# Two experts per engine loop turn on TensorE, buffers fixed by the expert's parity, extra passes behind expert 1

## The chip, the cores and the metric

One core of one Trainium2 chip runs the whole kernel. The metric is the device time of that core in microseconds (us), from one execution of the program. A run of this kernel repeats within 0.1%, so a median of a few runs tells changes of about 0.2% apart.

## What is computed

A decoder layer for 256 tokens of width 2048: a gated mixer over the sequence (two large projections, `a_w_in` 2048 x 4096 and `a_w_out` 2048 x 2048), then a mixture of 32 experts in 4 groups, then a final RMSNorm. All of it is float32. The mixture is the part that matters here:

```python
def hier_moe(h, w_group, b_group, w_exp, b_exp, w_gate, w_up, w_down):
    ...
    e_w, e_idx = lax.top_k(jax.nn.softmax(e_logits, axis=-1), TOP_K)      # TOP_K = 2
    ...
    def run_block(args):
        rows, e = args
        xb = x_pad[rows]
        return (jax.nn.silu(xb @ w_gate[e]) * (xb @ w_up[e])) @ w_down[e]
```

Each token goes to two of the 32 experts. An expert has three weight matrices of 2048 x 512 or 512 x 2048 float32, 4 MB each, 12 MB in all; the 32 experts have 384 MB, and each byte is used once.

## The kernel before

The program is written engine by engine; each engine has its own list of instructions and waits on named semaphores.

**Phase 1**, up to about 300 us, computes the mixer, with its weights split into a high and a low part, and then the router. TensorE's part of it holds one engine loop (`pe.Fori`, L1080) of two turns with two column blocks each.

**Phase 2** goes through the experts 0 to 31 in order. Each expert takes up to `CAP` = 32 tokens. On TensorE, `gather(e)` picks the tokens of the expert with a one-hot matrix, `transpose_xe(e)` turns them round, `gate_up(e)` multiplies them with gate and up weights in two halves, `transpose_gu(e)` turns the result, `down(e)` multiplies it with the down weights in two halves, and `scatter(e, t)` spreads the result over the tokens, one call for each of the two tiles of tokens. The gather of expert e+1 and the scatter of expert e-1 stand between the parts of expert e. ScalarE copies results out of PSUM, VectorE scales them and adds them to `acc`.

**The weights** come in chunks of 2 MB, six per expert and 192 in all: chunks 0 to 3 of an expert are gate, up, gate, up (two halves of the rows), chunks 4 and 5 are down. They are issued in order on one queue, SP's (`load_chunk`, L277). There are ten buffers of 2 MB (`slot`), and chunk 9 is put in the not yet used `acc`. `chunk_at(i)` gives the buffer of chunk i, and how many chunks have been in it before: from chunk 11 on the ten buffers are used in turn. SP waits before a load until TensorE has used the chunk that lay in the buffer before; the semaphore is one of four, counted by expert:

```python
e, c = divmod(i - NSLOT - (1 if i < IN_ACC + 1 + NSLOT else 0), NCH)
sp.wait_ge((gu_half, gu_half, gu_ps, gu_ps, y_half, y_ps)[c], e + 1)
```

`gu_half` and `gu_ps` come from TensorE at the end of the first and the second half of `gate_up`, `y_half` and `y_ps` at the end of the halves of `down`.

**Extra passes.** An expert with more than 32 tokens gets the rest in extra passes, whose number is known only at run time. GpSimd counts them, VectorE lists them (`list_passes`, L944), then TensorE, ScalarE and VectorE read the number and branch round the loop of passes if it is zero, as it is with these inputs. This stands behind expert `BREAK` - 1 = 15. There the pipeline of experts is emptied: `expert_run(0, BREAK)` ends with both scatters of expert 15, and `expert_run(BREAK, NEXP)` starts with the gather of expert 16, where elsewhere the gather of the next expert comes before `down`.

Of the kernel before, what the change touches and what calls it, by code (L numbers as in the profile page):

```python
# [20 lines left out]
def hybrid_layer(nc, x, norm_mix, norm_ffn, norm_final, w_in, ln_g, ln_b, w_s, b_s, w_out,  # L21
# [22 lines left out]
    IN_ACC = 9  # L44
    NCHUNK = NCH * NEXP

    MAXX = 16
    BREAK = NEXP // 2
    XUSED = 2 * KD + FT * NB
    XIN = 16 * XUSED  # L50
    assert (NT, KD, NB, FT, NQ, GD, NGRP * EPG, FE) == (2, 16, 4, 4, 4, 256, NEXP, 512)
# [1 line left out]
    with ExitStack() as ctx:  # L53
# [166 lines left out]
                return w[0, e, a * D // 2:(a + 1) * D // 2, :].rearrange("(p k) n -> p k n", k=8)  # L220
            return e_down[0, e, (c - 4) * 256:(c - 3) * 256, :].rearrange("(p b) n -> p b n", b=2)

        def chunk_at(i):

            if i < IN_ACC:
                return i, 0
            if i == IN_ACC:
                return NSLOT, 0
            if i == IN_ACC + 1:
                return NSLOT - 1, 0  # L230
            n = i - (IN_ACC + 2)
            return n % NSLOT, n // NSLOT + 1

        def chunk_tile(i):
            where = (slot + [acc[:, :, :].rearrange("p t d -> p (t d)")])[chunk_at(i)[0]]
            return where[:, :].rearrange("p (k n) -> p k n", k=8 if i % NCH < 4 else 2)

        def wait_chunk(pe, i):
            s, before_it = chunk_at(i)
            pe.wait_ge(chunk_in[s], 16 * (before_it + 1))  # L240
            if i in (IN_ACC + 2, IN_ACC + 3):
                pe.wait_ge(first_part[i - IN_ACC - 2], 16)

        def extra_passes(eng, body):

# [22 lines left out]
        @block.sync  # L268
        def _(sp):
            def load_half(src, n, hc, fresh=False):  # L270

                if not fresh:
                    sp.wait_ge(lo_done, HC * n + hc - 3)
                sp.dma_start(w_raw[:, hc % 4, :, :], src).then_inc(raw_in[hc % 4], 16)

            def load_chunk(i):
                sp.dma_start(chunk_tile(i), expert_chunk(i)).then_inc(chunk_in[chunk_at(i)[0]], 16)  # L277

            for q in range(NB):
                cols = slice(q * NBLK, (q + 1) * NBLK)  # L280
                sp.dma_start(h[:, :, cols], x[0, :, cols].rearrange("(t p) d -> p t d", p=P)).then_inc(x_in[q], 16)
                load_half(w_in_half(D, q), 0, q, fresh=True)

            for n in range(2 * NB):
                col = D + n * NBLK if n < NB else (n - NB) * NBLK
                for hc in range(4 if n == 0 else 0, HC):
                    load_half(w_in_half(col, hc), n, hc)
                if 1 <= n <= 3:
                    load_chunk(n - 1)
                if n == NB + 2:  # L290
                    sp.wait_ge(ln_done, NT * NB)
                    load_chunk(3)
                if n == NB + 3:
                    load_chunk(4)
            for n in range(NB):
                for hc in range(HC):
                    load_half(w_out_half(n * NBLK, hc), 2 * NB + n, hc)
                if n == 0:
                    sp.wait_ge(yt_ps, KD // 2)
                    load_chunk(5)  # L300
                if n == 1:
                    load_chunk(6)
            sp.wait_ge(w_used, 3 * NB * HC - HC // 2)
            load_chunk(7)
            sp.wait_ge(lo_done, 3 * NB * HC)
            load_chunk(8)
            sp.wait_ge(w_used, 3 * NB * HC)
            load_chunk(9)
            load_chunk(10)

            sp.wait_ge(gu_quarter, 1)
            for i in (IN_ACC + 2, IN_ACC + 3):
                half = 1 if i % NCH >= 4 else 4
                sp.dma_start(chunk_tile(i)[:, 0:half, :], expert_chunk(i)[:, 0:half, :]
                             ).then_inc(first_part[i - IN_ACC - 2], 16)
            sp.wait_ge(gu_half, 1)
            for i in (IN_ACC + 2, IN_ACC + 3):
                half = 1 if i % NCH >= 4 else 4
                sp.dma_start(chunk_tile(i)[:, half:2 * half, :], expert_chunk(i)[:, half:2 * half, :]
                             ).then_inc(chunk_in[chunk_at(i)[0]], 16)  # L320
            for i in range(IN_ACC + 4, NCHUNK):

                e, c = divmod(i - NSLOT - (1 if i < IN_ACC + 1 + NSLOT else 0), NCH)
                sp.wait_ge((gu_half, gu_half, gu_ps, gu_ps, y_half, y_ps)[c], e + 1)
                if i < NCHUNK - 1:
                    load_chunk(i)
                else:
                    for b in range(2):
                        sp.dma_start(chunk_tile(i)[:, b, :], expert_chunk(i)[:, b, :]
                                     ).then_inc((chunk_in[chunk_at(i)[0]], last_in)[b], 16)  # L330
            sp.wait_ge(gu_ps, NEXP - 1)
            sp.dma_start(g_final, norm_final.rearrange("(a d) -> a d", a=1).partition_broadcast(P)).then_inc(final_in, 16)

            for t in range(NT):
                for j in range(2):
                    sp.wait_ge((out_ready, out_ready_act)[j], t + 1)
                    cols = slice(j * D // 2, (j + 1) * D // 2)
                    sp.dma_start(out[0, t * P:(t + 1) * P, cols], acc[:, t, cols]).then_inc(out_stored, 16)
            sp.wait_ge(out_stored, 16 * NT * 2)
# [674 lines left out]
        def _(pe):  # L1014
# [172 lines left out]
            pe.matmul(R[:, COUNTS], ones_bf[:, :], mask[:, 1, :], start=False, stop=True).then_inc(ranks_ps, 1)  # L1187
            keep_busy(3)

            def gather(e):  # L1190
                if e == 0:
                    pe.wait_ge(sel_first, 1)
                else:
                    pe.wait_ge(sel_ready, e + 1)
                    pe.wait_ge(scatT_ready, e)
                for t in range(NT):
                    if e == 0 and t == 1:
                        pe.wait_ge(sel_ready, 1)
# [2 lines left out]
                                        start=(t == 0), stop=(t == NT - 1))  # L1201
                ins.then_inc(xe_ps, 1)

            def transpose_xe(e):
                pe.wait_ge(xe_ready, e + 1)
                if e:
                    pe.wait_ge(xeT_ready, e)
                for b in range(KC):
                    ins = pe.transpose(TRX[:, b * P:(b + 1) * P], xe.rearrange("p (c k) -> p k c", k=KC)[:, b, :],  # L1209
                                       ident[:, :])  # L1210
                ins.then_inc(xeT_ps, 1)
                pe.wait_ge(scat_ready, e + 1)
                for t in range(NT):
                    ins = pe.transpose(XE[:, t * P:(t + 1) * P], scat[:, t, :, :].rearrange("p q c -> p (q c)"), ident[:, :])
                ins.then_inc(scat_ps, 1)

            def gate_up(e):
                pe.wait_ge(xeT_ready, e + 1)
                if e:
                    pe.wait_ge(hT_ready, e)  # L1220
                for a in range(2):
                    tiles = [chunk_tile(NCH * e + 2 * a), chunk_tile(NCH * e + 2 * a + 1)]
                    wait_chunk(pe, NCH * e + 2 * a)
                    wait_chunk(pe, NCH * e + 2 * a + 1)
                    for k in range(8):
                        for c in range(NQ):
                            ins = pe.matmul(GU[c * CAP:(c + 1) * CAP, 0:256], xeT[:, k % KC, 2 * a + k // KC, :],  # L1227
# [3 lines left out]
                            ins.then_inc(gu_quarter, 1)  # L1231
                    ins.then_inc((gu_half, gu_ps)[a], 1)

            def transpose_gu(e):
                pe.wait_ge(gu_ready, e + 1)
                for b in range(2):
                    ins = pe.transpose(TRG[:, b * P:(b + 1) * P], gu.rearrange("p (c b) -> p b c", b=2)[:, b, :],
                                       ident[:, :])
                ins.then_inc(tr_ps, 1)

            def down(e):
                pe.wait_ge(hT_ready, e + 1)
                if e:
                    pe.wait_ge(y_ready, e)
                for c in range(2):
                    i = NCH * e + 4 + c
                    wait_chunk(pe, i)
                    for b in range(2):
                        if i == NCHUNK - 1 and b == 1:
                            pe.wait_ge(last_in, 16)  # L1250
# [3 lines left out]
                                            start=(c == 0 and b == 0), stop=(c == 1 and b == 1))  # L1254
                    ins.then_inc((y_half, y_ps)[c], 1)

            def scatter(e, t):
                if t == 0:
                    pe.wait_ge(y_ready, e + 1)
                    pe.wait_ge(scatT_ready, e + 1)  # L1260
                if NT * e + t:
                    pe.wait_ge(acc_done, NT * e + t)
                for j in range(NB):
                    rows_j = slice(j * CAP, (j + 1) * CAP)
                    ins = pe.matmul(O[j], scatT[rows_j, e % 2, t, :], y_sb[rows_j, :], start=True, stop=True)  # L1265
# [9 lines left out]
                        pe.matmul((O, O_LAST)[t][j][:, :], scatT[rows_j, e % 2, t, :], y_sb[rows_j, :],  # L1275
                                  start=True, stop=True).then_inc(scattered, 1)

            def expert_run(lo, hi):
                gather(lo)
                transpose_xe(lo)  # L1280
                for e in range(lo, hi):
                    gate_up(e)
                    if e > lo:
                        scatter(e - 1, 0)
                    if e + 1 < hi:
                        gather(e + 1)
                    transpose_gu(e)
                    if e + 1 < hi:
                        transpose_xe(e + 1)
                    if e == NEXP - 1:  # L1290
                        scatter(e - 1, 1)
                    down(e)
                    if e > lo and e < NEXP - 1:
                        scatter(e - 1, 1)
                if hi < NEXP:
                    scatter(hi - 1, 0)
                    scatter(hi - 1, 1)
                else:
                    last_scatter(hi - 1)

            def extra_pass(i):
                pe.wait_ge(x_sel, i + 1)
# [40 lines left out]
                    ins.then_inc(x_scattered, 1)  # L1343

            pe.sem_inc(x_used, 1)
            expert_run(0, BREAK)
            pe.wait_ge(passes_ready, 1)
            extra_passes(pe, extra_pass)
            expert_run(BREAK, NEXP)


# [20 lines left out]
```

## Time and profile before

| | |
|---|---|
| median of 3 runs | 1239.74 us (1239.44 to 1240.37) |
| the profiled execution | 1239.77 us |
| its span, first to last instruction | 1238.0 us |
| TensorE matmuls busy | 930.7 us, 7775 matmuls and as many weight loads |
| VectorE, ScalarE, GpSimd busy | 378.5, 223.3, 28.4 us |
| mean granted TensorE clock | 0.868 of full speed |
| moved by DMA | 462.33 MB, mean 373 GB/s |

The profile lists instructions by engine with start and duration, DMA traffic by queue, and the chain of waits that ended last. Times within it count from the first instruction; 1.8 us of the execution lie outside the span. A stretch of the profile can be asked for with its own numbers, so that a queue or an engine can be read for some microseconds alone.

### The profile page before, as it was taken

The page shows a single profiled execution, that of the slowest core. Times are in us where ns is not written, and L with a number is a line of the kernel's source. Part 1 is how long each engine was busy: PE and PEld are TensorE (multiplying, and loading weights), DVE is VectorE, ACT ScalarE, POOL GpSimd, SP SyncE. Part 2 cuts the span into 40 slices and gives each one's busy share as a digit, 9 for nine tenths or more (in the row PEclk, how much of TensorE's full clock was granted, in tenths as well). Part 3 has the DMA queues.
Part 4 walks back from the last instruction along what each step waited for, and adds up shares of the span by engine and source line. Part 5 has one row for each costly group of instructions (what it writes and reads, how often), then busy time and mean ns, then how long its engine had stood idle before and what let it go on. Part 6 is the DMA issues. An engine that isn't in the chain of part 4 may idle for free.

```text
span 1238.0 us, 17396 instructions
## 1 busy us (share of the span) xinstructions
PE 930.7 (75%) x7775; PEld 526.7 (43%) x7775; DVE 378.5 (31%) x479; ACT 223.3 (18%) x380; POOL 28.4 (2%) x60
## 2 busy tenths in 40 slices
PE   7999999999976767767777763866676667666674
PEld 6788788887433333333333321322233323322331
DVE  4554746445222222222222214222222222222214
ACT  5644555434100000000000000100000000000003
POOL 1100000000200000000000000000000000000003
PEclk9999999999997887887787886978878878888877
DMA  8877567857999999999999999999999999999993
GB/s 261 320 251 264 186 212 256 297 171 276 373 426 427 427 427 426 427 428 427 426 427 427 426 428 425 425 429 427 426 428 427 427 428 424 428 427 427 427 418 128
DMA packets 56811, 462.33 MB, mean 373 GB/s; under 512 B 4984, under 2 KB 5088, under 8 KB 31392
## 3 DMA queue, kind: packets, MB, share of 16 engines
q1 hardware_dynamic: 56000, 458.25, 90.6%
q0 software_dynamic: 656, 2.94, 0.7%
q8 instruction: 62, 1.02, 0.3%
q14 instruction: 13, 0.11, 0.0%
q10 hardware_dynamic: 80, 0.02, 0.0%
HBM read 459.09 MB, written 2.10 MB: 373 GB/s over the span
## 4 chain that ended last, share of the span: by engine, by line
DMA 55%; PE 39%; ACT 2%; DVE 2%; POOL 1%; issue 1%; POOLq 0%; SPq 0%; ACTq 0%; DVEq 0%
DMA slot<-in_e_w_up 54%; PE scattered_out L1049 19%; PE bank L1227 8%; PE bank L1252 5%; PE bank L1200 2%; PE scattered_out L1265 1%; PE bank L1209 1%; DMA w_raw<-in_a_w_out 1%; ACT arena L581 1%; POOL h L416 1%; DVE w_lo L680 1%; ACT w_hi L430 1%; PE bank L1093 1%; DMA w_raw<-in_a_w_in 0%; PE bank L1139 0%
## 5 line engine op out<-in xcount | busy, mean ns | idle before, releaser
L1227 PE MATMUL bank<-slot,arena 128*32 128x256 f32 x4064 | 343.8, 511 | 248.3 <-DMA slot<-in_e_w_up 247.1
L1227 PEld LDWEIGHTS bank<-slot,arena 128*32 128x32 f32 x4064 | 186.5, 145 | 415.0 <-issue 382.5
L922 DVE TENSOR_TENSOR acc<-scattered_out,acc 128x2048 f32<-128x2048 f32 x60 | 137.5, 2292 | 638.1 <-PE scattered_out L1265 638.1
L680 DVE TENSOR_TENSOR w_lo<-w_raw,w_hi 128x1024 fp32r<-128x1024 f32 x96 | 118.8, 1238 | 129.9 <-ACT w_hi L430 129.7
L1049 PE MATMUL scattered_out<-w_hi,xT_first 128*128 128x512 f32 x384 | 126.7, 400 | 3.4 <-DVE xT_first L689 1.9
L430 ACT CAST w_hi<-w_raw 128x1024 fp32r<-128x1024 f32 x96 | 100.9, 1051 | 138.0 <-PE scattered_out L1049 130.6
L1049 PE MATMUL scattered_out<-w_hi,xT_second 128*128 128x512 f32 x376 | 122.0, 396 | 0.5 <-DVE w_lo L680 0.5
L1252 PE MATMUL bank<-slot,arena 128*32 128x512 f32 x1024 | 116.5, 595 | 2.2 <-DVE arena L916 2.2
L591 ACT COPY arena<-bank 128x256 f32<-128x256 f32 x32 | 11.9, 372 | 563.5 <-PE bank L1227 563.5
L1049 PEld LDWEIGHTS scattered_out<-w_hi,xT_first 128*128 128x128 f32 x384 | 72.8, 190 | 22.1 <-issue 2.8
L1049 PEld LDWEIGHTS scattered_out<-w_hi,xT_second 128*128 128x128 f32 x376 | 70.6, 188 | 17.1 <-DVE w_lo L680 0.9
L1265 PE MATMUL scattered_out<-arena 32*128 32x512 f32 x496 | 71.7, 648 | 6.9 <-DVE acc L922 6.9
L1049 PE MATMUL scattered_out<-w_lo,xT_first 128*128 128x512 f32 x192 | 75.6, 394 | 0.0
L1049 PE MATMUL scattered_out<-w_lo,xT_second 128*128 128x512 f32 x188 | 73.4, 390 | 0.0
L1200 PE MATMUL bank<-h,arena 128*32 128x512 f32 x512 | 62.9, 610 | 13.4 <-issue 13.4
L1252 PEld LDWEIGHTS bank<-slot,arena 128*32 128x32 f32 x1024 | 30.0, 109 | 65.6 <-issue 62.1
L602 ACT COPY arena<-bank 128x512 f32<-128x512 f32 x32 | 18.7, 585 | 177.5 <-PE scattered_out L1265 163.6
L1049 PEld LDWEIGHTS scattered_out<-w_lo,xT_first 128*128 128x128 f32 x192 | 36.5, 190 | 6.7
L1265 PEld LDWEIGHTS scattered_out<-arena 32*128 32x128 f32 x496 | 19.6, 185 | 45.4 <-issue 40.0
L1049 PEld LDWEIGHTS scattered_out<-w_lo,xT_second 128*128 128x128 f32 x188 | 35.4, 188 | 6.3
L1200 PEld LDWEIGHTS bank<-h,arena 128*32 128x32 f32 x512 | 13.8, 110 | 56.9 <-issue 55.7
L581 ACT COPY arena<-bank 128x512 f32<-128x512 f32 x32 | 18.7, 585 | 99.4 <-PE bank L1200 99.4
(176 smaller groups left out, 416.6 us busy)
## 6 DMA issues: line engine op xcount, KB each, us to landing
slot<-in_e_w_gate SPq DMA_DIRECT2D x63, 2048.0 KB, 39.9
slot<-in_e_w_up SPq DMA_DIRECT2D x63, 2048.0 KB, 44.3
slot<-in_e_w_down SPq DMA_DIRECT2D x62, 2048.0 KB, 39.1
w_raw<-in_a_w_in SPq DMA_DIRECT2D x64, 512.0 KB, 4.0
w_raw<-in_a_w_out SPq DMA_DIRECT2D x32, 512.0 KB, 4.2
slot<-in_e_w_down SPq DMA_DIRECT2D x4, 1024.0 KB, 25.0
h<-in_x SPq DMA_DIRECT2D x4, 512.0 KB, 7.2
acc<-in_e_w_up SPq DMA_DIRECT2D x1, 2048.0 KB, 10.3
```

Source lines behind the costliest of these rows:

```text
L416: pool.tensor_tensor(h[:, t, cols], acc[:, t, cols], g_final[:, cols], ALU.mult).then_inc(acc_g_done, 1)
L430: act.copy(w_hi[:, hc % 2, :, :], w_raw[:, hc % 4, :, :]).then_inc(hi_done, 1)
L581: act.copy(xe, XE[:, :]).then_inc(xe_ready, 1)
L602: act.copy(y_sb, Y[:, :]).then_inc(y_ready, 1)
L680: dve.tensor_tensor(w_lo[:, hc % 2, :, :], w_raw[:, hc % 4, :, :], w_hi[:, hc % 2, :, :].bitcast(F32), ALU.subtract).then_inc(lo_done, 1)
L922: dve.tensor_tensor(acc[:, t, :], OUT[:, :], (acc if e else h)[:, t, :], ALU.add).then_inc(acc_done, 1)
L1049: ins = pe.matmul(Z[parity][t][:, :], a(k)[:, toks], b[:, hc % 2, j, :], start=(k == 0 and part == 0), stop=(k == KD - 1 and part == 2))
L1093: ins = pe.matmul(X[i % 4][:, j * GD:(j + 1) * GD], ws_T[:, g + j, :], v[:, t, (g + j) * GD:(g + j + 1) * GD], start=True, stop=True)
L1200: ins = pe.matmul(XE[j * CAP:(j + 1) * CAP, :], sel[:, e % 2, t, :], gather_columns(t, j), start=(t == 0), stop=(t == NT - 1))
L1227: ins = pe.matmul(GU[c * CAP:(c + 1) * CAP, 0:256], xeT[:, k % KC, 2 * a + k // KC, :], tiles[c // 2][:, k, (c % 2) * 256:(c % 2 + 1) * 25 ...
L1252: ins = pe.matmul(Y[j * CAP:(j + 1) * CAP, :], hT[:, b, c * CAP:(c + 1) * CAP], chunk_tile(i)[:, b, j * NBLK:(j + 1) * NBLK], start=(c == ...
L1265: ins = pe.matmul(O[j], scatT[rows_j, e % 2, t, :], y_sb[rows_j, :], start=True, stop=True)
```

## The change

- TensorE's experts 4 to 29 become an engine loop (`pe.Fori`) of 13 turns with two experts each. The waits in it count from registers (`2 * m + ...`). Experts 0 to 3, 30 and 31 stay written out.
- For that every turn must name the same buffers: from chunk 12 on, the six chunks of an even expert lie in the buffers 1, 2, 3, 4, 5, 6 and those of an odd one in 7, 8, 9, 0, 5, 6. Both take their down chunks in 5 and 6. SP waits for the last chunk that lay in the same buffer.
- `BREAK` becomes 2: the extra passes, and the emptied pipeline round them, stand behind expert 1 on all three engines.

SP's list stays written out, and the order of the chunks stays. The core of the diff:

```diff
-    BREAK = NEXP // 2
+    LOOP, LAST_LOOP = 4, 30
+    EVEN_SLOTS, ODD_SLOTS = (1, 2, 3, 4, 5, 6), (7, 8, 9, 0, 5, 6)
+    BREAK = 2
...
+        def buffer_of(i):
+            if i < IN_ACC:
+                return i
+            if i == IN_ACC:
+                return NSLOT
+            if i == IN_ACC + 1:
+                return NSLOT - 1
+            if i == IN_ACC + 2:
+                return 0
+            return (EVEN_SLOTS, ODD_SLOTS)[i // NCH % 2][i % NCH]
+
+        earlier = [[j for j in range(i) if buffer_of(j) == buffer_of(i)] for i in range(NCHUNK)]
+
         def chunk_at(i):
-            if i < IN_ACC:
-                return i, 0
...
-            n = i - (IN_ACC + 2)
-            return n % NSLOT, n // NSLOT + 1
+            return buffer_of(i), len(earlier[i])
...
-                e, c = divmod(i - NSLOT - (1 if i < IN_ACC + 1 + NSLOT else 0), NCH)
+                e, c = divmod(earlier[i][-1], NCH)
                 sp.wait_ge((gu_half, gu_half, gu_ps, gu_ps, y_half, y_ps)[c], e + 1)
...
+            def wait_chunk(i, m=0):
+                s, before_it = chunk_at(i)
+                per_turn = 16 if i % NCH < 4 else 32
+                pe.wait_ge(chunk_in[s], per_turn * m + 16 * (before_it + 1))
...
-            def gate_up(e):
-                pe.wait_ge(xeT_ready, e + 1)
+            def gate_up(e, m=0):
+                pe.wait_ge(xeT_ready, 2 * m + (e + 1))
...
-            def expert_run(lo, hi):
...
+            def other_experts():
+                gather(BREAK)
+                transpose_xe(BREAK)
+                for e in range(BREAK, LOOP):
+                    expert(e, first=(e == BREAK))
+                with pe.Fori(0, (LAST_LOOP - LOOP) // 2) as m:
+                    expert(LOOP, m=m)
+                    expert(LOOP + 1, m=m)
+                for e in range(LAST_LOOP, NEXP):
+                    expert(e, last=(e == NEXP - 1))
+                last_scatter(NEXP - 1)
...
-            expert_run(0, BREAK)
+            first_experts()
             pe.wait_ge(passes_ready, 1)
             extra_passes(pe, extra_pass)
-            expert_run(BREAK, NEXP)
+            other_experts()
```

The order of instructions shows two places. The first is SP's queue at the down chunks of experts 3 and 4; each row is one load of 2 MB with the semaphore that it waits for. Before:

```order
40 L277 DMA slot0<-in_e_w_up 128x4096 [waits y_ps]
41 L277 DMA slot1<-in_e_w_down 128x4096 [waits gu_half]
42 L277 DMA slot2<-in_e_w_down 128x4096 [waits gu_half]
43 L277 DMA slot3<-in_e_w_gate 128x4096 [waits gu_ps]
44 L277 DMA slot4<-in_e_w_up 128x4096 [waits gu_ps]
45 L277 DMA slot5<-in_e_w_gate 128x4096 [waits y_half]
```

The same place after the change:

```order
40 L280 DMA slot0<-in_e_w_up 128x4096 [waits y_ps]
41 L280 DMA slot5<-in_e_w_down 128x4096 [waits y_half]
42 L280 DMA slot6<-in_e_w_down 128x4096 [waits y_ps]
43 L280 DMA slot1<-in_e_w_gate 128x4096 [waits gu_half]
44 L280 DMA slot2<-in_e_w_up 128x4096 [waits gu_half]
45 L280 DMA slot3<-in_e_w_gate 128x4096 [waits gu_ps]
```

Row 40 is chunk 21, the last of the gate and up chunks of expert 3, and is the same in both. Row 41 is chunk 22. It waited for the first half of `gate_up(2)`, and waits now for the first half of `down(2)`; all later loads stand behind it.

The second place is TensorE behind `down` of expert 1 (`chunk_in9` and `chunk_in0` are its two down chunks). Before:

```order
904 L1252 MATMUL bank<-slot,arena 32x512 [waits chunk_in9,y_ready,hT_ready]
905 L1252 MATMUL bank<-slot,arena 32x512 x7
906 L1252 MATMUL bank<-slot,arena 32x512 [waits first_part0,chunk_in0]
907 L1252 MATMUL bank<-slot,arena 32x512 x7
908 L1265 MATMUL scattered_out<-arena 128x512 [waits acc_done]
909 L1265 MATMUL scattered_out<-arena 128x512 x3
910 L1227 MATMUL bank<-slot,arena 32x256 [waits first_part1,chunk_in1,chunk_in2,hT_ready,xeT_ready]
```

The same place after the change:

```order
900 L1262 MATMUL bank<-slot,arena 32x512 [waits first_part0,chunk_in0]
901 L1262 MATMUL bank<-slot,arena 32x512 x7
902 L1275 MATMUL scattered_out<-arena 128x512 [waits acc_done]
903 L1275 MATMUL scattered_out<-arena 128x512 x3
904 L1275 MATMUL scattered_out<-arena 128x512 [waits acc_done,scatT_ready,y_ready]
905 L1275 MATMUL scattered_out<-arena 128x512 x3
906 L1275 MATMUL scattered_out<-arena 128x512 [waits acc_done]
907 L1275 MATMUL scattered_out<-arena 128x512 x3
908 L249 TENSOR_LOAD n_extra_i [waits passes_ready]
909 L249 ISA x2
910 L250 COMPARE_AND_BRANCH
```

Where `gate_up(2)` followed one scatter, there are now three scatters, the read of the number of passes and the branch; then come the gather and the transposes of expert 2, which stood before `down(1)`, and only then `gate_up(2)`.

## Rows read from the trace of the kernel before

**Rows 1.** The page: TensorE and DMA in 40 slices, DMA queues, chain
```profile
span 1238.0 us, 17396 instructions
PE 930.7 (75%) x7775; PEld 526.7 (43%) x7775; DVE 378.5 (31%) x479; ACT 223.3 (18%) x380; POOL 28.4 (2%) x60
...
DMA  8877567857999999999999999999999999999993
...
q8 instruction: 62, 1.02, 0.3%
...
DMA 55%; PE 39%; ACT 2%; DVE 2%; POOL 1%; issue 1%; POOLq 0%; SPq 0%; ACTq 0%; DVEq 0%
```

**Rows 2.** The chain of waits in time (start us, us, what), first and last loads
```profile
342.26 30.73 DMA slot<-in_e_w_up
...
1158.69 46.25 DMA slot<-in_e_w_up
1204.94 0.14 issue
```

**Rows 3.** DMA queues from 373 to 1205 us: packets, MB, share of 16 engines
```profile
q1 hardware_dynamic: 24412, 354.30, 100.3%
q8 instruction: 46, 0.75, 0.4%
q14 instruction: 6, 0.05, 0.0%
```

**Rows 4.** Windows: us, engines busy (x instructions), clock, DMA share, GB/s
```profile
1204.00:1206.00 2.00, 0.93 (x12) 0.56 (x16) 0.00 (x0) 0.00 (x0) 0.00 (x0) 0.53 0.93 393
1206.00:1208.00 2.00, 2.00 (x24) 1.03 (x20) 0.00 (x0) 0.00 (x0) 0.00 (x0) 0.50 0.62 262
1208.00:1210.00 2.00, 2.00 (x24) 1.13 (x20) 0.00 (x0) 0.00 (x0) 0.00 (x0) 0.50 0.53 221
1210.00:1212.00 2.00, 2.00 (x24) 0.90 (x20) 0.00 (x0) 0.33 (x1) 0.00 (x0) 0.77 0.50 209
1212.00:1214.00 2.00, 1.11 (x10) 0.32 (x2) 1.26 (x1) 0.87 (x3) 0.00 (x0) 1.00 0.51 209
1214.00:1216.00 2.00, 0.91 (x8) 0.31 (x8) 1.23 (x2) 0.93 (x2) 0.00 (x0) 1.00 0.39 156
```

**Rows 5.** Windows in phase 1, the engine loop of L1080 within the second
```profile
28.00:84.00 56.00, 54.71 (x244) 44.11 (x243) 28.57 (x29) 30.62 (x35) 5.26 (x9) 1.00 0.84 298
84.00:152.00 68.00, 67.70 (x296) 54.67 (x295) 43.34 (x47) 32.42 (x38) 0.00 (x0) 1.00 0.67 222
```

**Rows 6.** DMA queues from 28 to 84 us
```profile
q1 hardware_dynamic: 5553, 14.33, 72.4%
q0 software_dynamic: 446, 2.31, 11.2%
q8 instruction: 3, 0.05, 0.4%
```

**Rows 7.** DMA queues from 84 to 152 us, all of them
```profile
## 3 DMA queue, kind: packets, MB, share of 16 engines
q1 hardware_dynamic: 6888, 15.11, 66.9%
issues: line engine op xcount, KB each, median us to landing
```

**Rows 8.** SP's queue in time at `down(15)`, and at `down(16)`
```profile
741.84 0.33 SPq L277 DMA_DIRECT2D slot<-in_e_w_up  x1
...
782.33 0.33 SPq L277 DMA_DIRECT2D slot<-in_e_w_gate  x1
```

**Rows 9.** TensorE and VectorE in time, behind expert 15
```profile
748.90 2.09 PE L1265 MATMUL scattered_out<-arena 32*128 32x512 f32 x8 [2.41 <-DVE acc L922]
...
756.58 0.17 DVE L956 TENSOR_SCALAR pass_rank<-pass_t 128x16 f32<-128x16 f32 x1
...
764.38 3.29 PE L1200 MATMUL bank<-h,arena 128*32 128x512 f32 x16 [13.39 <-issue]
```

**Rows 10.** GpSimd's last instruction of the count of extra passes
```profile
319.16 0.19 POOL L408 CAST n_extra_i<-rx 128x1 int32<-128x1 f32 x1
```

**Rows 11.** A load issued at 295.63 us, with nothing in the queue
```profile
slot<-in_e_w_gate SPq DMA_DIRECT2D x1, 2048.0 KB, 7.9
```

**Rows 12.** TensorE in time in expert 5: second half of `gate_up`, then `down`
```profile
432.24 5.35 PE L1227 MATMUL bank<-slot,arena 128*32 128x256 f32 x64 [4.46 <-DMA slot<-in_e_w_up]
...
442.12 3.64 PE L1252 MATMUL bank<-slot,arena 128*32 128x512 f32 x32
```

More of the change, by code:

```diff
@@ L221, in expert_chunk @@
             return e_down[0, e, (c - 4) * 256:(c - 3) * 256, :].rearrange("(p b) n -> p b n", b=2)
-        def chunk_at(i):
-            if i < IN_ACC:
-                return i, 0
[L227 to L230, printed above, removed]
-            n = i - (IN_ACC + 2)
-            return n % NSLOT, n // NSLOT + 1
+        def buffer_of(i):
[9 more added lines that the diff above has]
+        earlier = [[j for j in range(i) if buffer_of(j) == buffer_of(i)] for i in range(NCHUNK)]
+        def chunk_at(i):
+            return buffer_of(i), len(earlier[i])
         def chunk_tile(i):
@@ L236, in chunk_tile @@
             return where[:, :].rearrange("p (k n) -> p k n", k=8 if i % NCH < 4 else 2)
[L238 to L242, printed above, removed]
         def extra_passes(eng, body):
@@ L1188, in _, with gather @@
             keep_busy(3)
-            def gather(e):
+            def gather(e, m=0):
                 if e == 0:
@@ L1193, in gather @@
                 else:
-                    pe.wait_ge(sel_ready, e + 1)
-                    pe.wait_ge(scatT_ready, e)
+                    pe.wait_ge(sel_ready, 2 * m + (e + 1))
+                    pe.wait_ge(scatT_ready, 2 * m + e)
                 for t in range(NT):
@@ L1202, in gather, with transpose_xe @@
                 ins.then_inc(xe_ps, 1)
-            def transpose_xe(e):
-                pe.wait_ge(xe_ready, e + 1)
+            def transpose_xe(e, m=0):
+                pe.wait_ge(xe_ready, 2 * m + (e + 1))
                 if e:
-                    pe.wait_ge(xeT_ready, e)
+                    pe.wait_ge(xeT_ready, 2 * m + e)
                 for b in range(KC):
@@ L1211, in transpose_xe @@
                 ins.then_inc(xeT_ps, 1)
-                pe.wait_ge(scat_ready, e + 1)
+                pe.wait_ge(scat_ready, 2 * m + (e + 1))
                 for t in range(NT):
@@ L1215, in transpose_xe @@
                 ins.then_inc(scat_ps, 1)
-            def gate_up(e):
-                pe.wait_ge(xeT_ready, e + 1)
+            def wait_chunk(i, m=0):
+                s, before_it = chunk_at(i)
+                per_turn = 16 if i % NCH < 4 else 32
+                pe.wait_ge(chunk_in[s], per_turn * m + 16 * (before_it + 1))
+                if i in (IN_ACC + 2, IN_ACC + 3):
+                    pe.wait_ge(first_part[i - IN_ACC - 2], 16)
+            def gate_up(e, m=0):
+                pe.wait_ge(xeT_ready, 2 * m + (e + 1))
                 if e:
-                    pe.wait_ge(hT_ready, e)
+                    pe.wait_ge(hT_ready, 2 * m + e)
                 for a in range(2):
                     tiles = [chunk_tile(NCH * e + 2 * a), chunk_tile(NCH * e + 2 * a + 1)]
-                    wait_chunk(pe, NCH * e + 2 * a)
-                    wait_chunk(pe, NCH * e + 2 * a + 1)
+                    wait_chunk(NCH * e + 2 * a, m)
+                    wait_chunk(NCH * e + 2 * a + 1, m)
                     for k in range(8):
@@ L1232, in gate_up, with transpose_gu @@
                     ins.then_inc((gu_half, gu_ps)[a], 1)
-            def transpose_gu(e):
-                pe.wait_ge(gu_ready, e + 1)
+            def transpose_gu(e, m=0):
+                pe.wait_ge(gu_ready, 2 * m + (e + 1))
                 for b in range(2):
@@ L1239, in transpose_gu, with down @@
                 ins.then_inc(tr_ps, 1)
-            def down(e):
-                pe.wait_ge(hT_ready, e + 1)
+            def down(e, m=0):
+                pe.wait_ge(hT_ready, 2 * m + (e + 1))
                 if e:
-                    pe.wait_ge(y_ready, e)
+                    pe.wait_ge(y_ready, 2 * m + e)
                 for c in range(2):
                     i = NCH * e + 4 + c
-                    wait_chunk(pe, i)
+                    wait_chunk(i, m)
                     for b in range(2):
@@ L1255, in down, with scatter @@
                     ins.then_inc((y_half, y_ps)[c], 1)
-            def scatter(e, t):
+            def scatter(e, t, m=0):
                 if t == 0:
-                    pe.wait_ge(y_ready, e + 1)
-                    pe.wait_ge(scatT_ready, e + 1)
+                    pe.wait_ge(y_ready, 2 * m + (e + 1))
+                    pe.wait_ge(scatT_ready, 2 * m + (e + 1))
                 if NT * e + t:
-                    pe.wait_ge(acc_done, NT * e + t)
+                    pe.wait_ge(acc_done, 2 * NT * m + (NT * e + t))
                 for j in range(NB):
@@ L1276, in last_scatter, with expert, first_experts @@
                                   start=True, stop=True).then_inc(scattered, 1)
-            def expert_run(lo, hi):
[L1279 to L1299, printed above, removed]
+            def expert(e, first=False, last=False, m=0):
+                gate_up(e, m)
+                if not first:
+                    scatter(e - 1, 0, m)
+                if not last:
+                    gather(e + 1, m)
+                transpose_gu(e, m)
+                if not last:
+                    transpose_xe(e + 1, m)
+                if e == NEXP - 1:
+                    scatter(e - 1, 1, m)
+                down(e, m)
+                if not first and e < NEXP - 1:
+                    scatter(e - 1, 1, m)
+            def first_experts():
+                gather(0)
+                transpose_xe(0)
+                for e in range(BREAK):
+                    expert(e, first=(e == 0), last=(e == BREAK - 1))
+                scatter(BREAK - 1, 0)
+                scatter(BREAK - 1, 1)
+            def other_experts():
[9 more added lines that the diff above has]
+                last_scatter(NEXP - 1)
             def extra_pass(i):
```

## The prediction

> **What bounds the kernel now.** I read the page first: TensorE is busy 75% of the span, but the DMA engines are at nine tenths or more in every slice from the eleventh to the last but one, and the chain that ended last is 55% DMA [rows 1]. The chain in time then shows how: from the load of chunk 21, issued at 342.26 us and landed at 372.99, the chain runs through one load after another, to the up chunk 189 of expert 31 that lands at 1204.94 us [rows 2]. Behind it stand 33 us of tail, which the change leaves alone. So the end is set by one stream: 168 chunks in 831.95 us, 4.952 us each. TensorE matters only where it lets this stream run dry.
>
> Two more views tell what the stream is made of. Between 373 and 1205 us the weights' queue takes 100.3% of the 16 engines, and among its packets are 46 of the queue "instruction" q8 [rows 3]. q8 is TensorE's code: 62 packets of 16 KB for 15,550 matmuls and weight loads is one per 251 [rows 1]. The share of 0.4% would make it negligible. But the windows at the end show that it is not shared evenly: the DMA share falls to 0.62 at 1206 us and then stays at 0.50 to 0.53 until 1214 [rows 4]. Half of the 16 engines were done at about 1206, the other half at about 1215.5. A chunk has landed only when its slowest engine is done. My reading, not shown by any one row, is that the code packets go to eight of the engines and never to the other eight: those eight fell behind by some 9.5 us over 46 packets, 5.75 each, which is 1.65 us per packet on its engine (an estimate from these two numbers).
>
> **What the change removes.** 46 packets in the 28 experts of this stretch are 1.64 per expert. The loop's first turn must be fetched, the 12 others need not be if TensorE keeps the code of a turn: 24 experts x 1.64 = 39 packets fewer, 7 left. By the trace such a thing happens: with 487 TensorE instructions from 28 to 84 us there are three packets [rows 5, 6], with 591 instructions from 84 to 152 us, the second turn of the old loop within them, there is none [rows 5, 7]. That turn is 403 instructions, about 1.6 packets; the new turn is two experts, 3.3 packets. With 7 packets on 8 engines the slowest has one, where it had five or six: 9.5 - 1.65 = 7.9 us gained, by both bounds between 0 (code not kept) and 9.5 (no packet on the slowest). I take **-7.7 us**.
>
> **What the loop adds.** Some 26 register, wait and branch instructions per turn, on an engine that waits for DMA in every expert. In the old loop they left TensorE busy 67.70 of 68 us [rows 5]. Nothing, unless the stream runs dry.
>
> **The new break.** Behind expert 15, `down(15)` ended at 741.84 us (the load that waits for it) and the first half of `down(16)` at 782.33 [rows 8]: 40.5 us. In them lie three scatters with VectorE's additions between, the listing (to 756.75), then 7.6 us until the gather starts at 764.38 [rows 9]. All of it was hidden: ten chunks were outstanding. In the changed kernel the same chain stands behind `down(1)`, which ends at 342.26 us, as before [rows 2]; GpSimd's count is ready at 319.35 [rows 10]. The last scatter took 2.09 us behind expert 15 [rows 9]; behind expert 1 TensorE comes out of unbroken work and may do it in half of that. So the first half of `down(2)` ends at 342.26 + 40.5 - 0.5 = 382.3 us.
>
> That is what chunk 22 now waits for, in the order of SP's queue, and everything stands behind it. Chunk 21, the last one issued before, has landed at 372.99 us [rows 2]. **The queue runs dry.** A load into an idle queue took 7.9 us from issue to landing [rows 11], so chunk 22 lands at 390.2 us, where the stream without a gap has it at 372.99 + 4.95 = 377.9: **+12.3 us**. From below: if the 7.6 us to the gather shrink to 3, and the engines start at once, +6; from above, if reading, branching and code fetch take longer here, +15. Chunk 23 follows on `y_ps` 1.7 us later, inside the transfer of 22, and chunks 24 to 27 with it, since expert 2's gate and up are used; the stream is whole again.
>
> **The new order of buffers, later.** A down chunk of expert e+1 waits for `down(e)`. In the steady part the last up chunk of e has landed when the second half of `gate_up(e)` starts, and the first half of `down(e)` ends 442.12 + 1.82 - 432.24 = 11.7 us later [rows 12]; at the landing six more chunks are queued, 6 x 4.9 = 29 us. 17 us are left, in every turn and at experts 30 and 31. The other four chunks have more. Cost 0, and this cover also hides a stall at a turn's end of up to some 15 us.
>
> **The sum.** +12.3 - 7.7 = +4.6 us on the profiled execution's 1239.77 us, which is the median of the runs (1239.74) for this purpose: **1244.4 us**.
>
> **The rivals.**
>
> *A. The code of a turn isn't kept.* The old loop shows it for a turn half as long only. Then the 39 packets stay, and a turn that is entered anew may fetch more than it uses, at most one or two packets per turn, 13 to 26 in all, 2 or 3 on the slowest engine: 1239.77 + 12.3 + 0 to 5 = 1252 to 1257 us. The branch forward over the extra passes speaks for it: between the listing at 756.75 and the gather at 764.38 TensorE had nothing to wait for but its own code [rows 9]. The second turn of the old loop speaks against it [rows 7]. The Trainium skill, "Runtime: NRT & Kernel Launch", section "Instruction fetch mechanics", states both: that TensorE has room for 2048 instructions, by which a turn fits, and that a branch out of the current two pages of code has to fetch before it goes on. By the second sentence the sum would lose the 7.7 us and more; the trace agrees with it for the forward branch, and disagrees for the old loop. Chance 0.15.
>
> *B. The queue does not run dry* (the other side). If the first half of `down(2)` were done before about 370 us, chunk 22 would be queued in time, and only the gain is left: 1232.0 us. The point that decides is 12 us earlier than I reckon. For it speaks that the 13.39 us of idle time ahead of the gather [rows 9] include code fetch through a full DMA queue, which could be absent where the code lies otherwise. But of the 40.5 us only some 5 are of that kind. Chance 0.07.
>
> *C. Both terms are nearly equal.* With a break 4 or 5 us shorter (no code fetch at the branch), the stall is 7.5 us and the gain 7.7: 1239 to 1241 us. Chance 0.16.
>
> **How the numbers follow.** Forecast 0.62 (stall of 10.5 to 14, gain of 6.5 to 9: 1241.3 to 1247.5), A 0.15, B 0.07, C 0.16. A difference under 0.2% (2.5 us) can't be told from none. Of the forecast's 0.62 some 0.06 lies under that bound. Slower 0.56 + 0.15 + 0.03 of C's upper edge = 0.74; same 0.06 + 0.13 = 0.18; faster B and a little of C = 0.08. The range reaches over the forecast, C, and the lower edge of A: 1239 to 1253.
>
> **What would show it.** Right: DMA at nearly nothing for about ten microseconds from 372 us, while TensorE runs `gate_up(2)`; the first `down` of expert 2 late, its load issued at about 382; some 7 packets of q8 from 390 to 1208 us where there were 46; a cadence of 4.90 us per chunk (4.952 less 9.5 us over 168 chunks) instead of 4.95; the two halves of the DMA engines done within 2 or 3 us of each other at the end. Wrong: no empty stretch at 373 us (B), q8 with 60 packets or more (A), or a chunk cadence that stays at 4.95 though q8's packets are gone, by which the lag of eight engines would have another cause.

## The result and the profile after

| | before | after |
|---|---|---|
| median | 1240.24 us (7 runs, 1239.29 to 1241.25) | 1245.24 us (7 runs, 1244.18 to 1245.71) |
| ratio | | 1.0038, 95% interval 1.0028 to 1.0048 |
| span of the profiled execution | 1238.0 us | 1242.4 us |
| packets of q8, TensorE's code | 62 | 24 |

The change made the kernel slower by 0.38%, 5.0 us between the medians and 4.4 us between the profiled spans. The loop stands on TensorE alone, and q8's packets fall from 62 to 24 with it; written out again, the code has 62 packets. That shows that q8 carries TensorE's code, which the prediction took as given. Runs of one kernel differ by more than the three runs before the change suggested: 1239.29 to 1241.25 us here, and 1238.58 to 1241.73 (0.25%) in 17 runs beside the experiments.

The page after, its same parts as in [rows 1]:

```profile
span 1242.4 us, 17553 instructions
PE 935.2 (75%) x7775; PEld 521.5 (42%) x7775; DVE 378.7 (30%) x479; ACT 223.2 (18%) x380; POOL 28.4 (2%) x60
...
DMA  8877567858896999999999999999999999999994
...
q8 instruction: 24, 0.39, 0.1%
```

The busy times are nearly the same (TensorE 935.2 us for 930.7). The string of nines now has a gap, in the slice that begins at 373 us. SP's queue and the windows of the changed kernel show it (the windows' columns are as in [rows 4], the DMA share and GB/s last):

```profile
342.62 0.33 SPq L280 DMA_DIRECT2D slot<-in_e_w_up  x1
382.82 2.04 SPq L280 DMA_DIRECT2D slot<-in_e_w_down  x2
384.91 0.52 SPq L280 DMA_DIRECT2D slot<-in_e_w_gate  x1
```

```profile
366.00:372.00 6.00, 4.74 (x50) 1.96 (x46) 1.61 (x5) 0.96 (x2) 0.00 (x0) 0.84 0.76 317
372.00:374.00 2.00, 2.00 (x44) 1.24 (x40) 0.00 (x0) 0.00 (x0) 0.00 (x0) 1.00 0.00 0
...
380.00:382.00 2.00, 2.00 (x18) 1.08 (x22) 1.56 (x6) 0.07 (x1) 0.00 (x0) 1.00 0.00 0
382.00:384.00 2.00, 2.00 (x24) 0.65 (x20) 0.34 (x2) 0.00 (x0) 0.00 (x0) 1.00 0.59 106
...
1218.00:1220.00 2.00, 0.47 (x4) 0.31 (x8) 1.67 (x2) 1.37 (x2) 0.00 (x0) 1.00 1.00 418
1220.00:1222.00 2.00, 2.00 (x24) 0.51 (x20) 1.26 (x1) 0.00 (x0) 0.00 (x0) 1.00 0.45 184
1222.00:1224.00 2.00, 2.00 (x24) 0.43 (x16) 1.03 (x1) 0.00 (x0) 0.00 (x0) 1.00 0.01 4
```

Chunk 21 is issued at 342.62 us, chunk 22 at 382.82, and between 372 and 382 us the DMA engines do next to nothing (no slice of 2 us has a share above 0.04) while TensorE works almost without a pause: the wait is for its work, not for its idle time. The last three lines are the end of the weights: the share goes from 1.00 to nothing within some 2 us. In the kernel before it stood at about 0.50 for 8 us [rows 4].

TensorE between the two loads, in time:

```profile
349.67 2.09 PE L1275 MATMUL scattered_out<-arena 32*128 32x512 f32 x8 [2.40 <-DVE acc L925]
...
357.33 0.17 DVE L959 TENSOR_SCALAR pass_rank<-pass_t 128x16 f32<-128x16 f32 x1
...
364.69 3.49 PE L1203 MATMUL bank<-h,arena 128*32 128x512 f32 x16 [12.93 <-issue]
...
370.40 7.12 PE L1237 MATMUL bank<-slot,arena 128*32 128x256 f32 x128 [0.56 <-DVE arena L914]
```

It is the picture from behind expert 15 [rows 9]: the third scatter of 2.09 us, the listing, 7.2 us from the end of the listing to the gather (7.6 there). The load of chunk 22 landed 7.7 us after its issue, about 390.5 us.

DMA queues from 390 to 1209 us, and the last two pieces of the chain that are loads, with what follows:

```profile
q1 hardware_dynamic: 24051, 350.32, 100.6%
q8 instruction: 7, 0.11, 0.1%
```

```profile
1109.31 42.47 DMA slot<-in_e_w_up
1151.78 0.04 issue
...
1167.20 43.36 DMA slot<-in_e_w_up
1210.56 0.14 issue
```

Seven code packets where [rows 3] had 46: five up to 480 us, none from there to 1150, two behind. From 1151.78 to 1210.56 us twelve chunks land, 4.898 us each; over the whole stretch from chunk 22 to chunk 189 it is 4.91 us each, where the kernel before has 4.95.

So the time between the two profiled executions goes as follows. Chunk 22 lands at 390.5 instead of 377.9 us: +12.6. From there chunk 189 comes 1210.56 - 390.5 = 820.1 us later instead of 1204.94 - 377.9 = 827.0: -7.0. The tail behind it is 1242.4 - 1210.56 = 31.8 us instead of 33.1: -1.2. The sum is +4.4 us. The tail is shorter because the second half of `gate_up(31)` ran more of its time at the higher of TensorE's clock levels: 5.35 us after, 6.53 before. At other experts the same instructions take from 3.7 to 6.5 us before and from 4.9 to 6.5 after, so nothing ties these 1.2 us to the change. Before:

```profile
1205.07 6.53 PE L1227 MATMUL bank<-slot,arena 128*32 128x256 f32 x64 [3.50 <-DMA slot<-in_e_w_up]
```

After:

```profile
1210.69 5.35 PE L1237 MATMUL bank<-slot,arena 128*32 128x256 f32 x64 [4.56 <-DMA slot<-in_e_w_up]
```

The granted clock was 0.53, 0.50 and 0.50 in the slices from 1204 to 1210 us before [rows 4], and 0.74, 0.50 and 0.90 in those from 1210 to 1216 after.

### The profile page after: what moved, and what is told of

Same layout as the page of the kernel before. It is cut to its first block, busy times and chain, and to the rows that moved or that the text cites. A ratio compares the mean times of both kernels' runs of the same rounds, so it can differ in the third digit from the quotient of the medians.

```text
span 1242.4 us, 17553 instructions
## 1 busy us (share of the span) xinstructions
PE 935.2 (75%) x7775; PEld 521.5 (42%) x7775; DVE 378.7 (30%) x479; ACT 223.2 (18%) x380; POOL 28.4 (2%) x60
## 4 chain that ended last, share of the span: by engine, by line
DMA 49%; PE 42%; DVE 2%; ACT 2%; SPq 2%; issue 1%; POOL 1%; POOLq 0%; DVEq 0%; ACTq 0%
DMA slot<-in_e_w_up 49%; PE scattered_out L1052 20%; PE bank L1237 9%; PE bank L1262 5%; PE bank L1203 3%; SPq L280 2%; PE scattered_out L1275 2%; PE bank L1212 1%; DVE acc L925 1%; ACT arena L584 1%; POOL h L419 1%; PE bank L1096 1%; DVE w_lo L683 0%; DMA w_raw<-in_a_w_in 0%; PE bank L1142 0%
## 5 line engine op out<-in xcount | busy, mean ns | idle before, releaser
L1237 PEld LDWEIGHTS bank<-slot,arena 128*32 128x32 f32 x4064 | 180.8, 146 | 424.3 <-issue 334.3
L1262 PEld LDWEIGHTS bank<-slot,arena 128*32 128x32 f32 x1024 | 30.2, 110 | 67.0 <-issue 64.6
```

Of the source, the lines that this page charges most:

```text
L1262: ins = pe.matmul(Y[j * CAP:(j + 1) * CAP, :], hT[:, b, c * CAP:(c + 1) * CAP], chunk_tile(i)[:, b, j * NBLK:(j + 1) * NBLK], start=(c == ...
```

## The experiments

Theory T1 is the prediction's: a stall of the stream of about 12 us, and a gain that comes from code packets which load eight of the 16 DMA engines only. Eight kernels, each beside runs of the kernel before on the same chip: 17 runs with a median of 1239.94 us for the first four of them, 7 runs with 1240.44 us for the other four. The changed kernel's 1245.24 us stands beside 1240.24, so a difference between a kernel here and the changed kernel carries an error of some 0.5 us.

### The loop written out again

```diff
-                with pe.Fori(0, (LAST_LOOP - LOOP) // 2) as m:
-                    expert(LOOP, m=m)
-                    expert(LOOP + 1, m=m)
+                for e in range(LOOP, LAST_LOOP):
+                    expert(e)
```

> The changed kernel with its loop written out again (experts 4 to 29 unrolled), buffers by parity and the break behind expert 1 kept. Theory T1 (TensorE's code packets go to eight of the 16 DMA engines and cost each its 1.65 us): q8 back to 62 packets, the empty stretch of 372 to 384 us stays, chunk cadence back to 4.95 us, time 1245.2 + 7.7 = about 1253 us. Rival T2 (code packets cost only their share of all 16 engines, 0.1 us each): 1245.2 + 3.9 = about 1249 us. Rival T3 (the loop brought nothing): 1245 us.

Measured: 1253.20 us (4 runs), ratio to before 1.0107 (1.0092 to 1.0121). q8 has 62 packets again. The loop is worth 8.0 us, and rivals T2 and T3 fall. 8.0 us for 38 packets is 0.21 us per packet.

Not all of it is the stream. The profiled executions of the two kernels are 10.0 us apart. In this one chunk 22 lands at 392.1 us, 1.5 later, and chunk 189 at 1218.9: 826.8 us, 4.95 us per chunk again, where the changed kernel has 820.0. That is 6.8 us for 38 packets, 0.18 us each. The last 1.7 us are the tail (33.5 us for 31.8): `down(31)` took 5.31 us, at a granted clock of 0.50 from 1230 to 1232 us, where it took 3.62 at full clock in the changed kernel.

The end of the weights shows the half share again, in this kernel's windows:

```profile
1220.00:1222.00 2.00, 2.00 (x25) 0.98 (x21) 0.00 (x0) 0.00 (x0) 0.00 (x0) 0.50 0.91 385
1222.00:1224.00 2.00, 2.00 (x40) 1.14 (x32) 0.00 (x0) 0.00 (x0) 0.00 (x0) 0.94 0.51 213
1224.00:1226.00 2.00, 1.75 (x18) 0.63 (x10) 0.62 (x1) 0.59 (x2) 0.00 (x0) 1.00 0.50 209
1226.00:1228.00 2.00, 0.28 (x4) 0.28 (x8) 1.86 (x2) 1.55 (x3) 0.00 (x0) 1.00 0.52 205
```

How long the half share lasts can be read in every kernel's trace. The table gives the q8 packets from the last time that the queue stood empty (about 315 us, or the new gap) to the end of the weights, and the time between the end of the faster half of the engines and that of the slower (an estimate from the DMA share in slices of 0.5 us: what lies above 0.5 counts for the faster half):

| kernel | packets | us between the halves | us per packet |
|---|---|---|---|
| changed kernel | 8 | 1.5 | 0.19 |
| four experts per turn | 14 | 2.6 | 0.18 |
| break behind expert 3 | 17 | 2.8 | 0.17 |
| loop over experts 4 to 15 | 30 | 5.7 | 0.19 |
| written out | 46 | 8.1 | 0.18 |
| six experts per turn | 50 | 8.2 | 0.17 |
| kernel before | 52 | 8.8 | 0.17 |

The three kernels that the table leaves out fit in: 8 packets and 1.6 us (early listing), 17 and 3.0 (both), 47 and 8.2 (break behind expert 1 alone). The lag grows by 0.17 to 0.19 us with each packet, whatever the form of the code, and the stream pays nearly the same for one, 0.17 to 0.20 us here and below. The slower half sets the pace of the weights, and since its lag is as large as the price, the faster half can carry few of the packets or none. By this the engine that carries a packet loses some 1.4 us (an estimate, 8 x 0.18).

### The kernel before with the break behind expert 1 alone

```diff
-    BREAK = NEXP // 2
+    BREAK = 2
```

> The kernel before with BREAK = 2 alone: no loop, the ten buffers in turn as before. Chunk 22 then waits for the first half of gate_up(2), which ends some 9 us before the first half of down(2). T1: chunk 22 issued at about 374 us and landed at about 382 where the stream without a gap has it at 378, a stall of 4 us: 1244 us, 0.3% slower than before. If the whole 12 us of stall came from the break and not from the order of buffers, 1252 us. If the break costs nothing with the old order, 1240 us.

Measured: 1244.28 us (5 runs), ratio 1.0037 (1.0025 to 1.005). SP's queue and two windows of this kernel:

```profile
342.71 0.33 SPq L277 DMA_DIRECT2D slot<-in_e_w_up  x1
374.59 0.81 SPq L277 DMA_DIRECT2D slot<-in_e_w_down  x2
```

```profile
372.00:374.00 2.00, 2.00 (x44) 2.00 (x40) 0.00 (x0) 0.00 (x0) 0.00 (x0) 1.00 0.00 0
374.00:376.00 2.00, 2.00 (x45) 2.00 (x39) 0.00 (x0) 0.00 (x0) 0.00 (x0) 1.00 0.66 115
```

The stream is empty at 372 to 374 us and whole again from 378. The early break alone costs 4.3 us; the same break with the buffers by parity, and the same written-out code, costs 1253.2 - 1239.9 = 13.3 us. The order of buffers does 9 us of the stall, by the wait for `down(2)` in place of `gate_up(2)`: chunk 22 is issued at 374.59 us here and at 384.26 in the written-out kernel. The two parts of the change that were needed for the loop's form make this stall together.

### The break behind expert 3

```diff
-    LOOP, LAST_LOOP = 4, 30
+    LOOP, LAST_LOOP = 6, 30
-    BREAK = 2
+    BREAK = 4
```

> The changed kernel with the break behind expert 3 (BREAK = 4) and the loop over experts 6 to 29 (12 turns). There the queue reaches down to 432 us when the first half of down(4) ends at about 428. T1: no empty stretch, or one under 2 us; q8 about 27 packets; the gain alone is left: 1232 to 1234 us. If the stall comes with the break wherever it stands, 1245 us.

Measured: 1231.89 us (6 runs, five of them 1231.31 to 1233.15 and one 1238.06), ratio 0.9946 (0.9929 to 0.9963). q8 has 27 packets. Chunks 27 and 28 in SP's queue, and the windows at the point where the queue would end:

```profile
388.21 0.43 SPq L280 DMA_DIRECT2D slot<-in_e_w_up  x1
426.07 2.04 SPq L280 DMA_DIRECT2D slot<-in_e_w_down  x2
```

```profile
426.00:430.00 4.00, 4.00 (x65) 1.90 (x60) 0.00 (x0) 0.86 (x2) 0.00 (x0) 1.00 1.00 422
430.00:434.00 4.00, 2.76 (x56) 1.64 (x52) 0.00 (x0) 0.00 (x0) 0.00 (x0) 1.00 1.02 430
434.00:438.00 4.00, 4.00 (x60) 1.82 (x56) 0.78 (x1) 0.37 (x1) 0.00 (x0) 1.00 0.99 422
```

SP waits nearly as long as it did behind expert 1 (37.9 us for 40.2), and nothing is lost: chunk 27 landed 44.1 us after its issue, so the queue held loads up to about 432 us. In the changed kernel chunk 21 landed 29.8 us after its issue, and the queue reached only to 372. A likely reason, which no run isolates: TensorE begins expert 0 only at 308 us, with chunks that have long landed, and is still catching up behind expert 1. This version beats both kernels by the loop's gain.

### The listing of passes moved ahead

The break stays behind expert 1. On VectorE the listing comes while it has nothing to do:

```diff
                     make_hT(e)
+                    if e == BREAK - 1:
+                        list_passes()
...
             expert_run(0, BREAK)
-            list_passes()
```

> The changed kernel with VectorE's listing of the passes moved ahead, behind make_hT(1), into idle time. TensorE then reads the number right after the last scatter of expert 1, about 5.5 us sooner. T1 (each us of the break is a us of the empty stretch): chunk 22 issued at about 377 us, time 1245.2 - 5.5 = about 1239.7 us. Rival: if the time from the listing to the gather is code fetch alone and starts late, the gather does not move and the time stays at 1245.

Measured: 1238.33 us (11 runs), ratio 0.9983 (0.9974 to 0.9992). The break of TensorE in this kernel, in time:

```profile
351.69 2.09 PE L1276 MATMUL scattered_out<-arena 32*128 32x512 f32 x8 [2.40 <-DVE acc L925]
...
358.65 3.64 PE L1204 MATMUL bank<-h,arena 128*32 128x512 f32 x16 [4.88 <-issue]
```

The gather comes 7.0 us after the start of the third scatter instead of 15.0, and chunk 22 is issued at 378.21 us, 33.7 us after chunk 21, instead of 40.2. The gather is 8.1 us sooner, but 1.4 us are lost again: from the start of the gather to the end of `gate_up(2)` it takes 14.1 us in place of 12.6, at a granted clock of 0.50 up to 365 us and 0.89 behind, where the changed kernel has 0.72 and then 1.00. 6.5 us less of the break are 6.9 us less of the median. The two profiled executions say the same: chunk 22 issued 4.6 us sooner (this execution came to chunk 21 2 us later), span 4.7 us shorter. Within the stall, the break counts one to one. Between the last scatter and the gather 4.9 us of idle TensorE remain, with the reading, the branch and one q8 packet in them; no run separates the three.

### Both: break behind expert 3, early listing

> The break behind expert 3 and the early listing together. The break is covered by the queue there, so 5.5 us less of it are worth nothing: 1232 us, as with the break behind expert 3 alone (ratio to before 0.9946). If a hidden break still cost something, 1227 to 1230 us.

Measured: 1231.53 us (4 runs), ratio 0.993 (0.9913 to 0.9946). SP's queue at the same place:

```profile
389.31 0.43 SPq L280 DMA_DIRECT2D slot<-in_e_w_up  x1
421.88 2.04 SPq L280 DMA_DIRECT2D slot<-in_e_w_down  x2
```

The wait is 5.3 us shorter (32.6 for 37.9), and the median 0.4 us lower, less than the runs differ among themselves. What was worth 6.9 us behind expert 1 is worth nothing that can be told here.

### The loop over experts 4 to 15 alone

```diff
-    LOOP, LAST_LOOP = 4, 30
+    LOOP, LAST_LOOP = 4, 16
```

> The changed kernel with the loop over experts 4 to 15 alone (6 turns), 16 to 31 written out. The dose of the gain: 14 experts x 1.64 = 23 packets more than in the changed kernel, q8 about 47. T1 (eight DMA engines, 1.65 us per packet, the slowest counts): 3 packets more on the slowest, 1245.2 + 4.5 = about 1249.7 us. If the gain came from something else in the loop's later turns, not in proportion.

Measured: 1250.12 us (4 runs), ratio 1.0075 (1.0058 to 1.0092), 46 packets. 22 packets more than in the changed kernel cost 4.9 us between the medians, 0.22 us each; the stream from chunk 22 to chunk 189 is 4.2 us longer (824.2 us for 820.0), 0.19 us each. DMA queues of this kernel, first from 480 to 750 us, within the loop's turns, then from 750 to 1210:

```profile
q1 hardware_dynamic: 7940, 115.59, 100.7%
...
q1 hardware_dynamic: 13453, 195.94, 100.3%
q8 instruction: 24, 0.39, 0.3%
```

No code packet within the loop, 24 after it. The gain goes with the packets, in proportion.

### Four and six experts per turn

The second kernel has 6 and `3 * m` in these places:

```diff
-                with pe.Fori(0, (LAST_LOOP - LOOP) // 2) as m:
-                    expert(LOOP, m=m)
-                    expert(LOOP + 1, m=m)
+                with pe.Fori(0, (LAST_LOOP - LOOP) // 4) as m:
+                    for e in range(LOOP, LOOP + 4):
+                        expert(e, m=2 * m)
...
-    LOOP, LAST_LOOP = 4, 30
+    LOOP, LAST_LOOP = 4, 28
```

> The changed kernel with four experts per turn, experts 4 to 27 in 6 turns (28 to 31 written out). A turn is about 1650 instructions, 6.5 code packets. If TensorE keeps 2048 instructions (the Trainium skill): only the first turn is fetched, q8 about 24 + 3 + 3 = 30 packets, time about 1246 us. If it keeps fewer than 1650: q8 about 62 or more, time about 1253 us.

> The same with six experts per turn, experts 4 to 27 in 4 turns. A turn is about 2480 instructions, 9.7 code packets, more than 2048. If the capacity is 2048: all turns are fetched, q8 about 62 to 70, time about 1253 us, as unrolled. If it keeps more: q8 about 34, time about 1246 us.

Measured: four experts 1247.14 us (4 runs), ratio 1.0052 (1.0035 to 1.0068), 30 packets; six experts 1255.58 us (4 runs), ratio 1.012 (1.0103 to 1.0136), 66 packets. The DMA queues of the kernel with six, from 600 to 1100 us:

```profile
q1 hardware_dynamic: 14612, 212.80, 100.2%
q8 instruction: 30, 0.49, 0.4%
```

With four experts no q8 packet comes from 560 to 1100 us, with six there are 30 from 600 to 1100. So a turn of about 1650 instructions is fetched once, a turn of about 2480 in every turn, as if nothing were kept, and with four packets more than the code written out (66 for 62). The kernel with six has the loop, its registers and its order of buffers, and none of the gain: what the loop brings is the missing packets. These two kernels ran side by side, 8.4 us and 36 packets apart, 0.23 us per packet between the medians; in the stream it is 7.1 us, 0.20 each. The capacity of 2048 instructions that the Trainium skill gives ("Runtime: NRT & Kernel Launch", section "Instruction fetch mechanics") lies between the two; the trace agrees. Its sentence that a branch out of a window of two pages has to fetch does not hold for the backward branches of two and of four experts, which reach 3 and 6 packets of code back.

## Why the prediction was right

**The sum.** Forecast +4.6 us (1244.4), measured +5.0 between medians (1245.24) and +4.4 between the profiled executions, inside the range and with the forecast sign. Both terms were right in kind. That the profiled sum comes within 0.2 us is luck in part: the stall was 0.3 us larger, the gain 0.7 us smaller, and a tail that was forecast to stay gave 1.2 us. Rival A (code not kept) would have been near the kernel with six experts per turn, rival B near the break behind expert 3, and rival C near the early listing: each exists as a kernel, at 1255.6, 1231.9 and 1238.3 us, where they were reckoned at 1252 to 1257, 1232 and 1239 to 1241 (the last is 0.7 us below its range).

**The stall.** Forecast: chunk 22 issued at 382.3 us, landed at 390.2, +12.3. Measured: 382.82, 390.5, +12.6. The half microsecond that I took off for a quicker last scatter was wrong: it took 2.09 us again, at a granted clock of 0.50 behind expert 1 as behind expert 15. The break still was 40.2 us, 0.3 less than the 40.5 there, and it began 0.4 us later, at 342.62.

**The gain.** Forecast 7.7 us, with seven packets left. Measured 7.0 in the stream of the two profiled executions with seven packets left, 6.8 in the stream against the written-out loop, and 8.0 between the medians of those two. The price of a packet was set a little too high. I divided a lag of 9.5 us by the 46 packets behind 373 us, but the queue had last stood empty at about 315 us (the DMA share from 314 to 316 us is 0.08), and 52 packets came from then on. 9.5 us over 52 is 0.18 us per packet, 1.46 on its engine in place of 1.65 (the table above has 8.8 us for the same end, by finer slices, and so 0.17), and 39 packets at 0.18 are the 7.0 us that were measured.

That the code packets burden half of the DMA engines was a reading of the half share at the end. It now stands on the table above: the half share lasts as long as the packets are many, from 1.5 us for 8 packets to 8.8 for 52, with the same last loads in every kernel, so these loads are not its cause. Spread evenly over 16 engines, the packets would leave no such lag and 1.46 us would make 0.09 us per packet. Which engines they are, the profile doesn't show.

**Rival A's case.** The old loop was a weak witness against it. Its turn reaches 1.6 packets of code back, and a window of two may hold that, so the trace did not disagree there with the sentence of the Trainium skill that the prediction cites. The new loop, 3.3 packets long and without a packet from 480 to 1150 us, decides it.

**What I had at nothing.** The loop's own instructions: with q8 gone, twelve chunks at the end land every 4.898 us, as reckoned (4.90), so nothing of them can be told. The order of buffers in the steady part: no gap after 386 us, also nothing. The tail: I left it out, and it gave 1.2 us in this execution, by the clock.

**Two slips of the sums.** The upper edge of the forecast is 1239.77 + 14 - 6.5 = 1247.3 us, not 1247.5, and the chance of "same" adds up to 0.19, not 0.18. Neither changes the forecast.

## What to carry to other kernels

Where a stream of DMA sets the time, follow its queue: at each point ask up to when the loads already issued last, and which event of which engine releases the next one. The same pause of some 40 us in TensorE was worth nothing behind experts 3 and 15, 4.3 us behind expert 1 with one order of buffers and 13.3 with another. A load that is made to wait for a later release costs nothing in the steady part and 9 us in the first experts, where less is queued ahead (30 us behind expert 1, 44 behind expert 3). And a queue's small share is no measure of its price, if it falls on few engines that all must finish: from 373 to 1205 us TensorE's code had 0.4% of the 16 engines, and doing without 39 of its 46 packets gave back 7.0 us of these 832, 0.8%.

## What the runs showed of the hardware

- TensorE's code comes in packets of 16 KB, one per about 250 instructions, and takes room on the DMA engines that load weights: 0.17 to 0.20 us of the stream per packet, and the slower half of the engines falls behind by 0.17 to 0.19 us per packet. An estimate from it is 1.4 us on the engine that carries the packet. The packet's own transfer is shorter: in the kernel before, one packet has 3.4% of 16 engines in the window from 614 to 616 us, which is 1.1 us. The row of the DMA queues there:

```profile
q8 instruction: 1, 0.02, 3.4%
```

- A loop whose turn has about 830 or 1650 instructions is fetched once; one with about 2480 is fetched in every turn, at more packets than straight code.
- A load of 2 MB into an idle queue takes 7.4 to 7.9 us to land (seven such loads, in the kernel before and in six kernels with the stall), where the stream gives one every 4.9: each time that the queue runs dry costs some 3 us on top of the wait.
